# 32 unused floats ahead of the weight buffers of a two-layer fp32 trunk

## The reference

```python
def swiglu(x, w_gate, w_up, w_down):
    return (jax.nn.silu(x @ w_gate) * (x @ w_up)) @ w_down
...
    h = jnp.concatenate([meta, x], axis=1)
    for layer in range(DEPTH):
...
        h = h + FFN_RESIDUAL * swiglu(rmsnorm(h, norm_ff1[layer]), ff1_w_gate[layer],
                                      ff1_w_up[layer], ff1_w_down[layer])
        hn = rmsnorm(h, norm_mix[layer])
        if layer % 2 == 0:
            mix = conv_ssm_mixer(hn, even_w_in[idx], conv_w[idx], ssm_lambda_re[idx],
...
            mix = window_attention(hn, attn_w_qkv[idx], attn_q_norm[idx], attn_k_norm[idx],
...
        h = h + mix
        h = h + FFN_RESIDUAL * swiglu(rmsnorm(h, norm_ff2[layer]), ff2_w_gate[layer],
                                      ff2_w_up[layer], ff2_w_down[layer])
```

## Time and profile before

| what | before |
|---|---|
| median of 3 runs | 1881.71 us (1881.29 to 1882.42) |
| profiled execution, its own time | 1882.0 us |
| its span, first to last instruction | 1880.0 us |
| PE busy | 1865.3 us (99%) |
| PEld busy | 1765.6 us (94%) |
| DVE busy | 955.1 us (51%) |
| ACT busy | 599.6 us (32%) |
| POOL busy | 350.8 us (19%) |
| granted TensorE clock, mean | 0.998 of 2.4 GHz |
| transfers, mean over the span | 100 GB/s |

### The profile page before, as it was taken

The page is one execution under the profiler, slowest core; times in us unless marked ns, Lnnn a source line. Parts: engine busy times, 40 slices in busy tenths (PEclk is TensorE's granted clock), DMA queues, the critical chain, the costliest instruction groups (busy, mean ns, idle before and its releaser), DMA issues.

```text
span 1880.0 us, 33855 instructions
## 1 busy us (share of the span) xinstructions
PE 1865.3 (99%) x13887; PEld 1765.6 (94%) x13887; DVE 955.1 (51%) x1077; ACT 599.6 (32%) x707; POOL 350.8 (19%) x629
## 2 busy tenths in 40 slices
PE   8999999999999999999999999999999999999999
PEld 8999999999999999999999999999988788888887
DVE  5444356568765443344564443445556654434443
ACT  5222222332243222222342222223456442222232
POOL 2888889414330000000000000000012000000000
PEclk9999999999999999999999999999999999999999
DMA  7332444547523332433243323322321233333423
GB/s 183 90 84 84 142 147 128 163 126 185 137 69 90 90 84 84 120 82 83 70 126 90 84 84 101 90 81 71 112 73 46 62 96 92 92 94 104 110 70 87
DMA packets 330785, 188.29 MB, mean 100 GB/s; under 512 B 8152, under 2 KB 323832, under 8 KB 330712
## 3 DMA queue, kind: packets, MB, share of 16 engines
q1 hardware_dynamic: 323296, 166.81, 32.0%
q0 software_dynamic: 7088, 20.38, 4.0%
q10 hardware_dynamic: 328, 0.07, 0.0%
HBM read 174.91 MB, written 11.14 MB: 99 GB/s over the span
## 4 chain that ended last, share of the span: by engine, by line
PE 95%; DVE 2%; issue 1%; ACT 1%; DMA 1%; ACTq 0%; POOL 0%; SPq 0%; DVEq 0%
PE ps L799 78%; PE ps L1015 5%; PE ps L1057 2%; PE ps L1126 2%; PE ps L1076 1%; PE ps L1265 1%; PE ps L1227 1%; DMA raw<-in_ff_w_down 1%; PE ps L844 1%; PE ps L1167 0%; PE ps L976 0%; PE ps L975 0%; PE ps L966 0%; DVE r L1592 0%; DVE wl L1563 0%
## 5 line engine op out<-in xcount | busy, mean ns | idle before, releaser
L799 PE MATMUL ps<-xh,wh 128*128 128x264 f32 (+1 forms) x2432 | 557.7, 299 | 0.3 <-DVE t_a L1616 0.2
L799 PE MATMUL ps<-xh,wl 128*128 128x264 f32 (+1 forms) x2432 | 556.6, 298 | 0.0
L799 PE MATMUL ps<-xl,wh 128*128 128x264 f32 (+1 forms) x2432 | 556.6, 298 | 0.0
L1563 DVE TENSOR_TENSOR wl<-raw,wh 128x2048 fp32r<-128x2048 f32 x171 | 398.3, 2329 | 173.6 <-ACT wh L1276 173.6
L1276 ACT ACTIVATE wh<-raw 128x2048 fp32r<-128x2048 f32 x172 | 327.5, 1904 | 248.6 <-PE ps L799 205.7
L799 PEld LDWEIGHTS ps<-xh,wh 128*128 128x128 f32 x2432 | 384.9, 188 | 15.3 <-issue 1.4
L799 PEld LDWEIGHTS ps<-xl,wh 128*128 128x128 f32 x2432 | 384.8, 188 | 13.8 <-issue 0.2
L799 PEld LDWEIGHTS ps<-xh,wl 128*128 128x128 f32 x2432 | 384.8, 188 | 13.8
L799 PE MATMUL ps<-act_h,wh 128*128 128x264 f32 (+1 forms) x1232 | 282.2, 298 | 1.2 <-DVE wl L1563 1.2
L799 PE MATMUL ps<-act_h,wl 128*128 128x264 f32 (+1 forms) x1232 | 281.6, 298 | 0.0
L799 PE MATMUL ps<-act_l,wh 128*128 128x264 f32 (+1 forms) x1232 | 281.5, 298 | 0.0
(11 more groups left out here) (308 smaller groups left out, 1681.3 us busy)
## 6 DMA issues: line engine op xcount, KB each, us to landing
raw<-in_ff_w_gate SPq DMA_DIRECT2D x88, 512.0 KB, 4.0
raw<-in_ff_w_up SPq DMA_DIRECT2D x87, 512.0 KB, 5.2
raw<-in_ff_w_down SPq DMA_DIRECT2D x64, 384.0 KB, 4.0
raw<-in_ff_w_down SPq DMA_DIRECT2D x64, 320.0 KB, 3.7
raw<-in_even_w_in SPq DMA_DIRECT2D x16, 512.0 KB, 5.3
raw<-in_attn_w_qkv SPq DMA_DIRECT2D x12, 512.0 KB, 4.4
raw<-in_even_w_out SPq DMA_DIRECT2D x8, 512.0 KB, 4.5
raw<-in_attn_w_o SPq DMA_DIRECT2D x8, 512.0 KB, 4.6
```

The source lines that it names most:

```text
L799: last = nc.tensor.matmul(ps[:, 2 * pair + hf, 0:nh], w[:, slot, b * P:(b + 1) * P], x[:, k0 + k, c0 + hf * nh:c0 + (hf + 1) * nh], start= ...
L1563: v.tensor_tensor(wl[:, c % 2, :], raw[:, c % 2, :], wh[:, c % 2, :].bitcast(F32), ALU.subtract).then_inc(wl_ready, 1)
```

## The change

One more tile of 32 floats (128 bytes in each partition) is declared between `act_l` and `raw`. Nothing reads or writes it. Every tile declared behind it starts 128 bytes later; those ahead of it stay where they are. No instruction is added, removed or moved on any engine, and no shape or wait differs; only addresses do. The pad leaves the tiles' sizes alone and still fits in SBUF.

```diff
         act_h = sb("act_h", [P, PART[0], ROW], F32R)[:, :, 0:L]
         act_l = sb("act_l", [P, PART[0], ROW], F32R)[:, :, 0:L]
+        weight_pad = sb("weight_pad", [P, 32])
         raw = sb("raw", [P, 2, UNITW])
         wh = sb("wh", [P, 2, UNITW], F32R)
         wl = sb("wl", [P, 2, UNITW], F32R)
```

## The result

The changed kernel takes 1919.5 us (median of 4 runs, 1910.2 to 1920.7) against 1882.1 us (median of 4 runs of the kernel before, one more than above): 37.5 us slower. The profiled execution has a span of 1917.8 us. One run of a later kernel, with the weights alone moved, took 8733 us; it is left out of that kernel's median and ratio, and what held it up is not known.

The account below looks back on a forecast made before the run. It took TensorE's stream of matmuls, busy 99% of the span, to bound the kernel; all terms were 0, so the forecast was the unchanged median of 1881.7 us, likeliest range 1878 to 1885.5, with 1850 to 1905 leaving about 0.2 outside.

Parts of the forecast that it names:

- What bounds the kernel: TensorE's matmul stream: each matmul costs 10.1 or 13.5 ns more than its columns, 12,576 matmuls taking 92% of the span.
- 0.30 ns per matmul: Smallest visible effect on the 12,576 matmuls with a moved operand: 0.2% of the time, 3.8 us.
- a grid of 128 bytes or less: SBUF reads of TensorE's operands: cut at multiples of 128 bytes or less, starts 128 and 0 are alike; 0 us.
- (1): Term for 12,576 matmuls with a weight operand at 0 instead of 128: 0 ns each, at worst 6.4 ns each.
- two readings: TensorE operand reads are cut at multiples of 128 bytes (no change) or of 256 (128 already off the grid).
- third reading: TensorE's two operand starts count relative to each other, such as banks alternating every 128 bytes; no term in the sum.
- three pairs of starts: Moving/stationary at 512 columns: 128/128 (L799) 226.87 ns, 128/192 (L1076) 233.3 ns, 192/128 (L1126) 229.1 ns.
- The evidence against dependence within 256 bytes: Plain fp32 matmuls of L975 and L976 pass many relative starts yet keep 109.5 ns each; called weaker evidence.
- The relation 128 / 0 is worse: Rival on the weight matmuls: half a period apart costs time, 13 us (1895 us) to 80 us (1962 us); slower 0.22.
- argument for the small end: Halves of 264 columns start 32 bytes apart yet pace at 2 x 120.08 in all stages, favouring the smaller price.
- opposite rival: Weights half a period from the moving operand free the stream: at most 120 us, to 1762 us, value 1822 us; faster 0.20.
- VectorE, ScalarE and transfers: Term for their work on moved tiles: 0, as slack of 7.3 us per unit hides even 10%, 0.42 us per unit.

Follow-up runs that it names:

- the map: Kernels without the trunk, fp32r matmuls alone on tiles with chosen starts; at 512 columns 226.7 ns at distance 0, 232.2 at 128 (moving at 128).

## Why the prediction was wrong

**What bounds the kernel**: right. The loss is nowhere but in the distance from one matmul's start to the next. One of its sentences is too strong: the extra of 13.5 ns is not that of every stretch with 512 columns, since its own rows of L1126 and L1076 have 229.1 and 233.3 ns. The 0.30 ns per matmul that it took as the smallest visible loss was not put to the test: the loss came to 2.9 and 4.7 ns.

**The step that failed** is "That speaks for a grid of 128 bytes or less, and so for no change", and with it "(1) ... I take 0 ns each". It weighed two readings in which each operand has a good and a bad start of its own, showed that one of them fails, and took the other for established. The third reading, that "the two operands' starts count relative to each other", was named there, with the remark that "128 / 0 is a case that no row shows", and got a share of the 0.22 for a slower kernel, but no term in the sum. It was the right one: both moved together, 0.9998; either one moved alone, 1.0178 and 1.0197; and the map depends on the difference only. The three pairs of starts that the prediction listed were three distances, 0, 64 and 192, and all their values fit the map. The weights' 0 ns were 2.9 ns at 264 columns and 4.7 to 5.7 at 512.

**The evidence against dependence within 256 bytes** was the plain fp32 stream of the earlier trace rows. It differs from the stream of the weights in two ways. It streams at half the rate: the plain fp32 products with `ones` in the same trace (L809) follow each other every 222 ns with 264 columns. And it loads 66 stationary columns, not 128. Nothing measured here carries its indifference over to fp32r at full speed. That the extra of 10 ns was gone at 1.2 GHz was a hint that a slow stream may hide the distance, and for that clock the changed kernel shows it. Its first products (start us, us; then a window around them), at distance 128:

```profile
17.27 0.64 PE L845 MATMUL ps<-xh,wh 128*128 128x264 f32 x2
17.71 0.64 PE L845 MATMUL ps<-xl,wh 128*128 128x264 f32 x2
...
16.30:18.00 1.70, 1.70 (x8) 1.70 (x9) 1.70 (x3) 1.70 (x4) 1.70 (x2) 0.50 0.94 162
```

They take 0.44 us for two, 220 ns each, the same as at distance 0 in the earlier trace rows.

**The rivals.** "The relation 128 / 0 is worse" is what happened, in mechanism and place, with a price of 13 to 80 us; measured 37.5. Its argument for the small end does not carry: the halves of 264 columns put every second matmul of the kernel before at distance 224 and the others at 0, and this pair is among the cheapest of the map, 120.0 ns. That says nothing of 128, where the two halves lie at 128 and 96 and take 123.3 or 122.2. "Equal starts may be the best case" holds at 512 columns (226.7 ns is the least of eight), "half a period the worst" does not: 96 is dearer there (234.3). The opposite rival, that half a period frees the stream, fell: no stream that went from distance 0 to 128 became faster. L1077 did, but it went from 64 to 192.

**VectorE, ScalarE and transfers; `ident`, `ones`, `arena`**: right, 0 (0.9996 and 0.9995; and 0.9998 with every tile moved, `wh` and `wl` as ScalarE and VectorE write them included).

**The rule of the Trainium skill**, page "TensorE: Matmul & The Clock Gate", section "Step-by-step: what each phase is for": two independent read ports, and a load that takes no read bandwidth from the running matmul. The prediction drew from it that no start matters. This stream disagrees: the distance alone is worth 1.9% of the kernel. No run here tells what unit the two readers meet in.

**Not settled.** Why one distance has two paces (123.4 and 122.3 ns), what sets the pace for a given column count, and why a disturbance lasts longer at 264 columns than at 512. No version beat the kernel before: the starts that L1126 and L1076 lack would give 192 x 2.4 + 96 x 6.6 = 1.1 us, under what the measurement tells, and it was not tried.

## What to carry to other kernels

Where matmuls follow each other without a pause, read the distance from start to start against the columns' own time, and note the start of both operands modulo 256 bytes: it is their difference, not each one's alignment, that set the pace here, in fp32r streams at 2.4 GHz with a load for every matmul. A pad or a new tile ahead of one operand can cost 2% without adding an instruction, so at 264 and 512 columns keep stationary and moving tiles at equal starts (at 256 and 448 the distance 128 was the cheaper one), and check the built addresses after every change of the allocation. When two readings of the same rows remain after one is refuted, look for the rows that part the survivors before putting a price of zero.

## What the runs showed that was not expected

- With two halves of 264 columns, first-half distances of 0, 32, 64 and 96 cost nothing (120.0 to 120.1 ns) while 128 to 224 cost up to 3.3 ns; at 512 columns every distance but 0 costs 2.3 to 7.6 ns.
- Mismatched loads in one matmul of three cost 77% of what they cost in all.
- The kernels with all weights at distance 128 scatter: 1909.6 to 1923.9 us in four runs of the one with moved moving operands, 1910.2 to 1920.7 in four of the changed one, while 19 runs of the kernel before lie within 1879.8 to 1882.6. The two paces at 264 columns would explain it: an estimate from them is 10,560 x 1.1 ns = 12 us between a run with only one and a run with only the other. With `wl` or `wh` alone moved, where the trace has 122.28 ns, four runs each lie within 3.1 us.
- Distance 128 is cheaper than distance 0 at 448 columns (204.0 against 206.7 ns).
- At a granted clock of 0.50 the distance costs nothing: 220 ns for 264 columns at distance 0 and at distance 128.
